# Seven block products for the first layer's gates and for the convolution layer's last eight input tiles

## The reference, cut to what matters

```
mx = cond_x @ w_mod[layer] + b_mod[layer]             # one row of 3072 numbers a stream: the "mod columns"
hx = rmsnorm(x, g_pre) * (1 + scale_x) + shift_x      # the same for ctx
# layer 0, both streams (512 tokens):
cq, ckv, kr, gate = split(h @ w_in)                   # gate: 1024 columns
y = (attend(...) * silu(gate)) @ w_out
# layer 2, both streams:
p = h @ w_in                                          # 4096 columns: 24 tiles of 128 for u, 8 for the gate
u = short_conv(p[..., :3072])                         # three taps along the tokens, for each channel
y = (z(u) * silu(p[..., 3072:])) @ w_out
```

## Time and profile before

| what | value |
|---|---|
| runs | 1842.67, 1848.17, 1847.88 us; median 1847.88 |
| the profiled execution, its own time | 1843.65 us |
| its span in the trace | 1841.9 us, mean granted clock 0.997 |
| PE busy | 1791.9 us, 97% of the span |
| DVE busy | 902.1 us, 49% |
| ACT busy | 432.2 us, 23% |
| DMA | 367.59 MB |

### The profile page before, as it was taken

The page is one execution under the profiler, slowest core; times in us unless marked ns, Lnnn a source line. Parts: engine busy times, 40 slices in busy tenths (PEclk is TensorE's granted clock), DMA queues, the critical chain, the costliest instruction groups (busy, mean ns, idle before and its releaser), DMA issues.

```text
span 1841.9 us, 18562 instructions
## 1 busy us (share of the span) xinstructions
PE 1791.9 (97%) x6973; PEld 985.7 (54%) x6973; DVE 902.1 (49%) x2131; ACT 432.2 (23%) x1037; POOL 81.1 (4%) x94
## 2 busy tenths in 40 slices
PE   6999999999999999999999999999999999999997
PEld 2545564448554644583446845688854344343432
DVE  4873458887888666668974143363441001010001
ACT  2121242202762322212223232222021111111111
POOL 0000000000001000005500000000010000000000
PEclk9999999999999999999999999999999999999999
DMA  9652202362204333411123511443669999999993
GB/s 399 251 212 97 118 1 96 121 236 84 92 1 148 125 130 144 183 50 43 74 71 113 183 46 39 173 181 111 238 264 378 427 428 427 428 428 426 428 429 159
DMA packets 31400, 367.59 MB, mean 200 GB/s; under 512 B 3675, under 2 KB 3788, under 8 KB 6348
## 3 DMA queue, kind: packets, MB, share of 16 engines
q1 hardware_dynamic: 31308, 366.36, 49.8%
HBM read 365.26 MB, written 1.09 MB: 199 GB/s over the span
## 4 chain that ended last, share of the span: by engine, by line
PE 61%; DVE 4%; issue 1%; ACT 0%; POOL 0%; DVEq 0%; POOLq 0%; ACTq 0%
PE bank L3576 12%; PE bank L2354 8%; PE bank L3613 6%; PE bank L1115 5%; PE bank L3597 3%; PE bank L3551 3%; PE bank L1233 3%; PE bank L2874 2%; PE bank L1844 2%; PE bank L1681 2%; PE bank L3380 1%; PE bank L1375 1%; PE bank L2643 1%; PE bank L2877 1%; PE bank L1397 1%; PE bank L3200 1%
## 5 line engine op out<-in xcount | busy, mean ns | idle before, releaser
L426 DVE SCALAR_TENSOR_TENSOR product<-slot,cond_rows 128x1024 f32<-128x1024 f32 x160 | 199.4, 1246 | 14.1 <-DMA slot<-panels_dram 7.9
L2354 PE MATMUL bank<-hT,slot 128*128 128x512 f32 (+1 forms) x448 | 168.9, 531 | 0.0
L1115 PE MATMUL bank<-hT,slot 128*128 128x256 f32 (+1 forms) x576 | 156.4, 427 | 0.4 <-DVE open_o L1138 0.4
L3653 DVE SCALAR_TENSOR_TENSOR hT<-hT,bank 128x512 f32<-128x512 f32 x16 | 11.0, 688 | 259.8 <-ACT hT L3688 259.8
L1115 PEld LDWEIGHTS bank<-hT,slot 128*128 128x128 f32 x576 | 108.0, 190 | 40.0 <-issue 28.1
L2354 PEld LDWEIGHTS bank<-hT,slot 128*128 128x128 f32 x448 | 83.3, 190 | 70.5 <-issue 67.4
L3613 PE MATMUL bank<-slot,hT 128*64 128x512 f32 x256 | 92.1, 595 | 0.0
L3576 PE MATMUL bank<-slot,scratch 128*64 128x512 f32 x256 | 90.6, 592 | 0.0
L2136 PE MATMUL bank<-slot,hT 128*128 128x512 f32 x192 | 82.7, 592 | 0.0
L3613 PE MATMUL bank<-late_slots,hT 128*64 128x512 f32 x208 | 70.8, 595 | 1.0 <-ACT hT L3692 1.0
L3576 PE MATMUL bank<-late_slots,scratch 128*64 128x512 f32 x208 | 69.9, 592 | 0.0
(11 more groups left out here) (493 smaller groups left out, 3089.3 us busy)
## 6 DMA issues: line engine op xcount, KB each, us to landing
slot<-panels_dram SPq DMA_DIRECT2D x91, 2048.0 KB, 9.9
late_slots<-panels_dram SPq DMA_DIRECT2D x40, 2048.0 KB, 20.2
slot<-panels_dram SPq DMA_DIRECT2D x40, 1024.0 KB, 5.1
branch_slot<-panels_dram SPq DMA_DIRECT2D x9, 2048.0 KB, 23.0
mod_slot<-panels_dram SPq DMA_DIRECT2D x4, 2048.0 KB, 16.6
slot<-panels_dram SPq DMA_DIRECT2D x4, 1536.0 KB, 7.9
gate_rows_all<-gate_rows_dram SPq DMA_DIRECT2D x4, 1024.0 KB, 4.6
slot<-panels_dram SPq DMA_DIRECT2D x2, 1280.0 KB, 18.4
```

Source lines behind the costliest of these rows:

```text
L426: last = m.nc.vector.scalar_tensor_tensor(out=m.product[:], in0=m.slot(panel)[:, c * D:(c + 1) * D], scalar=1.0, in1=m.cond_rows[:, s, :], ...
L1115: last = self.m.nc.tensor.matmul(self.bank(g), self.m.slot(panel)[:, k * width + j * P:k * width + (j + 1) * P], self.m.hT[:, k, 0:self.n] ...
L2354: last = nc.tensor.matmul(bank(g)[:, tokens], m.slot(i)[:, k * 512 + g % 4 * P:k * 512 + (g % 4 + 1) * P], m.hT[:, k, tokens], start=k == ...
```

## The change

`ProductGates` gets hooks (`panel_and_tile`, `row`, `gate`, `low_taken`, `fourth_weights`, `third_rows`) and a subclass `ConvolutionProducts` with 8 pairs, in which both tiles of a pair come from one panel. In layer 2 the first 16 tiles stay whole; tiles 16 to 23 and the 8 gate tiles are one run of 8 pairs on panels 4 to 7. A tile pair's sum goes to `tmp` (SBUF, upper) and to the low bank (PSUM, lower), gets its centre tap from ACT, its side taps from DVE, and is transposed by PE behind SEVENTH and FOURTH of the next pair. In layer 0 the eight gate tiles are four pairs on panels 2 and 3, with the transposes behind named products; layer 3 keeps `Gates`. The mod columns are placed anew: in layer 0 they move back as far as the attention (seven there), in layer 2 three follow tile 0 and tiles 6 to 12, one follows tile 15, nine stand in the tile pairs.

```diff
+class ConvolutionProducts(ProductGates):
+    PAIRS, TILE_PAIRS = 8, 4
+    def panel_and_tile(self, n, j):
+        return self.panels[j // 2], 2 * (j % 2) + n
+    def row(self, j, upper):
+        if j < self.TILE_PAIRS:
+            return self.tmp[:, j % 2, :]
+        return self.m.gT[:, 2 * (j - self.TILE_PAIRS) + upper, :]
+    def low_taken(self, pe, j):
+        if j < self.TILE_PAIRS:
+            pe.wait_ge(self.conved.sem, self.conved.at(self.first_tile + 2 * j + 2))
...
 def attention(...):
+        @block.sync
+        def _(sp):
+            if columns:
+                columns.refill(sp, columns.panels - 4)
+                columns.refill(sp, columns.panels - 3)
...
+                    if columns and u >= 2 and s == 0:
+                        columns.some(dve, 1)
                     for q in range(NX):
                         dve.wait_ge(scored.sem, scored.at(at(u, q)))
...
 def latent_inputs(...):
-                    for i in (range(0, 5), range(5, 8))[n]:
+                    for i in ((0, 1), (2, 3))[n]:
                         columns.refill(sp, i)
...
                 gate_columns(m, dve, layer)
-                columns.some(dve, 16)
+                columns.some(dve, 2)
+            if by_products:
+                for i in panels[2:4]:
+                    dve.wait_ge(*m.loaded(i))
+                gates.sum_tokens(dve, "third")
+                gates.sum_weights(dve, 1, 0)
+                gates.sum_weights(dve, 2, 0)
+                dve.wait_ge(ready.sem, ready.at(len(groups)))
+                gates.sum_tokens(dve, "first")
+                gates.sum_tokens(dve, "second")
+                gates.sum_tokens(dve, "fourth")
+                gates.sum_weights(dve, 3, 0)
+                gates.sum_weights(dve, 4, 0)
...
+                for pair in range(4):
+                    gates.take(dve, pair, gates.SIXTH)
+                    if pair >= 2:
+                        columns.some(dve, 1)
+                    gates.take(dve, pair, gates.FIFTH)
...
+                    gates.take(dve, pair, gates.SEVENTH)
+                    if pair < 3:
+                        gates.sum_weights(dve, 3, pair + 1)
+                    if pair < 2:
+                        norm(2 * pair)
...
 def latent_qkv(...):
-                columns.some(dve, 2)
+                columns.some(dve, 9)
...
 def conv_inputs(...):
+        WHOLE = 16
+        tiles = list(range(WHOLE)) + [WHOLE + 2 * j + n for j in range(4) for n in (1, 0)]
+        columns_of = [3 if g == 0 or 6 <= g <= 12 else 2 for g in range(WHOLE - 1)] + [1]
+        columns_of_pair = (3, 2, 2, 2)
...
+            for n in range(4):
+                if n < 2:
+                    columns.refill(sp, 8 + n)
+                elif n == 2:
+                    columns.refill(sp, 10)
+                    columns.refill(sp, 11)
+                    m.issue(sp, filters.w3)
+                sp.wait_ge(gates.summed.sem, gates.sum_at((4, 2 * n + 1)))
+                sp.wait_ge(gates.ready.sem, gates.product(2 * n + 1, gates.THIRD))
+                m.load_next(sp, panels[4 + n])
...
                 for n in gates.following(j):
                     gates.matmuls(pe, j, n)
+                    if 1 <= j <= gates.TILE_PAIRS and n in (gates.SEVENTH, gates.FOURTH):
+                        turn(WHOLE + 2 * (j - 1) + (n == gates.FOURTH))
...
+                if j < gates.TILE_PAIRS:
+                    columns.some(dve, 1)
+                if j == gates.TILE_PAIRS:
                     dve.wait_ge(*m.loaded(filters.w3))
...
+                if j < gates.TILE_PAIRS:
+                    for upper in (True, False):
+                        side_taps(WHOLE + 2 * j + (not upper), gates.source(j, upper))
+                    columns.some(dve, columns_of_pair[j] - 1)
```

More of the change, by code:

```diff
@@ L1281, in take @@
     def take(self, dve, j, n):
-        v, kept, out = self.m.nc.vector, self.pair(self.kept[j % 2]), self.m.gT[:, 4 + j, :]
+        v, kept, out = self.m.nc.vector, self.pair(self.kept[j % 2]), self.row(j, True)
         middle, high, sixth, fifth = (self.pair(x) for x in (self.middle, self.high, self.sixth, self.fifth))
@@ L1823, in _ @@
                 gate_rows.spread(sp)
-            for n in range(2):
-                if columns:
-                    for i in ((8,), (9, 10, 11))[n]:
-                        columns.refill(sp, i)
-                sp.wait_ge(gates.ready.sem, gates.ready.at(4 * n + 4))
-                m.load_next(sp, panels[2 + n])
+            if by_products:
+                columns.refill(sp, 4)
+                columns.refill(sp, 5)
+                sp.wait_ge(gates.summed.sem, gates.sum_at((4, 3)))
+                sp.wait_ge(gates.ready.sem, gates.product(3, gates.SECOND))
+                m.load_next(sp, panels[2])
+                sp.wait_ge(gates.ready.sem, gates.product(3, gates.THIRD))
+                m.load_next(sp, panels[3])
+                columns.refill(sp, 6)
+            else:
+                for n in range(2):
+                    sp.wait_ge(gates.ready.sem, gates.ready.at(4 * n + 4))
+                    m.load_next(sp, panels[2 + n])
         @block.tensor
@@ new lines, in _ @@
+            if by_products:
+                for i in panels[2:4]:
+                    pe.wait_ge(*m.loaded(i))
+                for j, n in gates.OPENING:
+                    gates.matmuls(pe, j, n)
+                for j in range(4):
+                    for n in gates.following(j):
+                        gates.matmuls(pe, j, n)
+                        if (j, n) in turn_behind:
+                            turn(turn_behind[j, n])
+                    if j == 0:
+                        pe.wait_ge(read.sem, read.at(len(groups)))
+                        gate_rows.turn(pe)
+            else:
+                for g in range(8):
+                    i = panels[2 + g // 4]
+                    if g % 4 == 0:
+                        pe.wait_ge(*m.loaded(i))
+                    gates.matmuls(pe, g, i, g % 4)
+                    t = g - TURN_AFTER
+                    if t == -1:
+                        pe.wait_ge(read.sem, read.at(len(groups)))
+                    if 0 <= t < NT:
+                        turn(t)
@@ new lines, in _ @@
+            if by_products:
+                gates.keep_first(act, 0)
+                gates.keep_first(act, 1)
+                for pair, turns in enumerate(((), (0,), (1,), (2, 3))):
+                    if pair >= 2:
+                        gates.keep_first(act, pair)
+                    for t in turns:
+                        take_turned(t)
+                    gates.half_tangent(act, pair, True)
+                    gates.half_tangent(act, pair, False)
+                    if pair == 0:
+                        gate_rows.copy(act)
+            else:
+                for g in range(8):
+                    gates.half_tangent(act, g)
+                    t = g - TURN_AFTER
+                    if 0 <= t < NT:
+                        take_turned(t)
@@ L1955, in _ @@
                 m.load_next(sp, panels[n])
+                if columns:
+                    for i in ((9, 10), (11,), ())[n]:
+                        columns.refill(sp, i)
         @block.tensor
@@ L2041, in _ @@
                 if columns:
[L2042 removed]
+                    columns.some(dve, (8, 4)[n])
             for s, g in turns:
@@ L2364, in _, with turn @@
             m.tile_of_hT(pe, NT - 1)
-            for g in range(CH + 1):
-                if g < CH:
+            def turn(c):
+                pe.wait_ge(conved.sem, conved.at(c + 1))
+                if 2 <= c < KD + 2:
+                    pe.wait_ge(folded.sem, folded.at(c - 1))
+                elif c >= KD + 2:
+                    pe.wait_ge(read.sem, read.at(c - KD - 1))
+                for t in range(NT):
+                    last = nc.tensor.transpose(turn_bank(c)[:, t * P:(t + 1) * P], uc[:, c % 2, t * P:(t + 1) * P], m.ident[:, :])
+                last.then_inc(turned.sem, turned.one())
+            for g in range(WHOLE + 1):
+                if g < WHOLE:
                     i = panels[g // 4]
@@ L2451, in _ @@
                 last.then_inc(conved.sem, conved.one())
+            for g in range(WHOLE):
+                side_taps(g, bank(g)[:, :])
                 if 1 <= g <= KD:
```

341 lines of the change are left out of this document (196 added, 145 removed).

## The result

| | median us | runs | ratio to before (95%) |
|---|---|---|---|
| before, in the same comparison | 1847.6 | 6, 1842.67 to 1848.25 | |
| changed | 1854.69 | 6, 1853.21 to 1856.73 | 1.0041 [1.0029, 1.0053] |

The change makes the kernel 7 us slower, where 7.6 us faster was forecast. The profiled execution took 1854.92 us, its span is 1853.1 us at a mean granted clock of 0.992, against 1841.9 and 0.997.

A forecast was written before the change was run, and what follows sets the result against it. PE work was taken to count in full while VectorE and the loads keep up. Layer 0's -6.6 and layer 2's -1.0 us sum to -7.6, from 1845.6 to 1838.0 us; 8-in-10 range 1833 to 1846.5.

The forecast's parts named there:

- `filters.w3`: Layer 2, pair 4: its late load makes VectorE stand 3.2 us and delays SIXTH of pair 5; +1.4 us, bounds 0 and 3.7.
- Opening: Layer 2 after tile 15: one column ahead of the token sums starts SIXTH late; +0.7 us, bounds 0 to 1.3.
- three signs of being wrong: PE idle in layer 0's pairs, waits in pairs 2 to 4 not near zero, or the `filters.w3` load landing before T+10.
- T+10: 10 us after FOURTH's end behind pair 3, in layer 2; the `filters.w3` load was forecast to land at T+13.4.
- C: Rival: VectorE bounds the product runs, PE waiting 2.2 us at SEVENTH in seven further pairs; +7.8 us, 1853.4, chance 0.09.
- layer 0: Gates as four pairs of seven block products, VectorE and loads keeping up: -6.6 us, gates to `latent_qkv` in 51.5 us.
- attention: Seven columns moved into 2.35 us gaps where VectorE waits for PE in the attention; cost 0, 8.8 us without that cover.
- Start: Layer 2's first tiles: three columns instead of two after tile 0 delay PE's transposes; +1.3 us, bounds 0 to 1.3.
- pair 0 to pair 1: Layer 2: VectorE's taps and two columns delay the take of SIXTH, so SEVENTH waits; +2.2 us, bounds 0 and 3.3.
- pairs 1 to 3: Layer 2: VectorE takes SIXTH before PE needs SEVENTH; 0, with up to 1 us a pair as the bad end.
- Layer 2: Product saving -6.6 us, less waits of 1.3, 0.7, 2.2 and 1.4 us: -1.0 us.
- Rival A: Layer 2's four waits are shorter, 2 us in all instead of 5.6: -11.2 us, time 1834.4, chance 0.12.

The follow-up runs named there:

- the loads ahead: Changed kernel with only SyncE's sixth and eighth column-panel loads of layer 2 issued ahead of the waits for PE's tiles 11 and 15; 1840.12 us, ratio 0.9965.
- the columns placed for it: Changed kernel with column-panel loads issued early, layer 2's columns placed anew, and pair 1's SIXTH taken between pair 0's side taps; 1832.74 us, ratio 0.9916.
- the columns spread: Changed kernel, SyncE's list kept, layer 2 columns re-placed: three after tiles 0, 8, 13, 14 and in each tile pair, two after other tiles; 1843.65 us.
- the load behind: Against the kernel with the loads ahead, only the eighth column panel's load moved back behind the wait for tile 15 and the 2 MB load; 1858.07 us.
- the load between: Against the kernel with the loads ahead, only the eighth column panel's load moved behind the wait for tile 15 but ahead of the 2 MB load; 1847.09 us.

## Why the prediction was wrong

*The step that failed* is the condition in the first paragraph, "as long as VectorE and the loads keep up", taken as met for layer 2's tiles 6 to 15. Tiles 6 to 14 have no term in the sum at all. The working checked VectorE's time behind tile 15 and in the pairs, and the one load that the diff moved, `filters.w3`; it did not ask when SyncE's list issues the column panels that a pace of three a tile needs. The term "Opening", +0.7 with bounds 0 to 1.3, has in its place 10.18 + 2.65 us of waits (0.64 of it stays when the load is early), 1.14 before the transposes of tiles 12 and 13, and some 2.6 us at the lower clock (transposes +0.5, SIXTH 3.55 instead of 1.80, the next product 2.02 instead of 1.73). With 0.16 for each of the three extra waits, that is 16.4 of the 16.5 us between the two stretches (223.91 against 207.39); between the medians it is 14.6. What was needed was there: the order of the loads in SyncE's list, and the new `columns_of`. No rival named it, and none of the three signs of being wrong came (waits in layer 0's pairs, waits in pairs 2 to 4, a load before T+10; it landed near T+13): they watched the places that had a term. C has the right sign and nearly the right time, 1853.4, by another mechanism, and the takes of pairs 2 to 4 did not wait.

*What was right*, in order: layer 0, 51.5 us forecast, 51.53 measured, its ratio alone 0.9964; attention 0, measured -0.04; Start +1.3, measured 1.21 (9.97 us from the first to the third transposes against 8.76); Opening, once the load is early, 0.7 forecast and 0.64 listed; pair 0 to pair 1, 2.2 and 2.17; pairs 1 to 3, no wait; `filters.w3`, VectorE stands 3.2 and 3.22, PE 1.4 and 1.50. From the end of tile 15 to the end of the products 107.5 us were forecast; with the loads ahead it is 108.2, in the changed kernel 123.1. For the load of `filters.w3` the measured landing held: 7.65 us in the chain of the changed kernel. The estimated 6.8 us by the fit of the Trainium skill (DMA: Bandwidth & Descriptors, Anatomy of one DMA) is too short here. Layer 2 was forecast at -1.0 us in all; with the loads ahead its stretch is 0.4 shorter than before. The kernel that I forecast exists: it is the one with the loads ahead, 1840.12 us, where 1838.0 was forecast.

*The level* was 2 us too low: the first profile of before was of an execution with both of the places just shown short, and the median of 17 runs is 1847.4, not the mean of four, 1845.6.

*Rival A's gain* (-11.2) was out of reach of the change as written, but not of the form. With the columns placed for it the medians are 15 us apart. The profiles account for 13.9 of them: 6.6 in layer 0, and 7.3 in the stretch of layer 2, which is more than the 6.6 of its products since the old 0.81 wait goes too. Executions with the same mean granted clock, 0.997, are 13.5 us apart (1829.5 against 1843.0), so about 1 us of the 15 is in which executions each median falls on.

## What to carry to other kernels

When an engine's work is moved earlier, walk the issue list of what it consumes: for each load, which wait and which transfer stand ahead of it, and at what point of the consumer it is then needed. An in-order issue list has a pace of its own, set by another engine's progress, and no busy share in the profile before showed how near it was. A long stall of PE costs its waits and then a tail at the lower clock, here 2.6 us behind 10.2; and waits that an added load of work brings can often be had back by moving the same work by one step.

## What the runs showed of the hardware

After 10 us without work PE's matmuls came back at half speed. Granted clock by windows of 5 us, the changed kernel (us, PE busy, clock, DMA share, GB/s):

```profile
720.00:725.00 5.00, 0.82 (x4) 1.00 0.98 416
725.00:730.00 5.00, 0.00 (x0) 0.53 0.39 165
730.00:735.00 5.00, 1.34 (x5) 0.50 0.00 0
735.00:740.00 5.00, 5.00 (x15) 0.61 0.00 0
740.00:745.00 5.00, 5.00 (x25) 1.00 0.00 0
```

The columns are PE's busy time, the granted clock, the DMA share and GB/s. The level is 0.50, 1.2 GHz, and eight PE instructions of 128 x 256 take 3.75 us there instead of 1.89. After 5.19 us without work it was the same (3.75). Behind waits of 0.5 to 2.4 us the products of layer 2 show 1.97, with two exceptions: 3.21 with the columns spread, where a wait of 2.16 us began 14 us after one of 2.14 had ended, and 3.65 with the load behind, where one of 2.17 us began 17 us after the stall. In the profiles of the changed kernel and of the load between the same wait of 2.17 us, 16 us after a stall, did not bring it (1.97), nor did 2.17 us behind 0.64 with the loads ahead. That the clock after a short wait is not a property of the kernel alone is shown by the kernel before: behind the same wait of 1.97 us, the clock was 1.00 in one execution and 0.67 in the other.

A load of 1 MB landed after 5.1 us alone and 9.8 us when issued 0.4 us behind one of 2 MB, itself 7.7 us. With the load between it is the other way round: the 1 MB took 5.2 us, and the 2 MB behind it 9.7. In both the landings came in the order of issue, and the load behind paid for the one ahead.
